# Expert biases of a mixture-of-experts block: copied into the accumulators by ScalarE instead of added by TensorE, GpSimd and VectorE

## The chip, the cores and the metric

One Trainium2 chip, one of its cores in use. The metric is the device time of one launch, in microseconds (us). Engines are named as the profile names them: PE (TensorE), DVE (VectorE), ACT (ScalarE), POOL (GpSimd), SP (SyncE, which here only issues DMAs). PSUM is the memory that PE accumulates into, eight banks of 512 fp32 numbers on each of 128 partitions.

## The reference, cut to what matters

One encoder block on 512 tokens of width 1024: a mixer (recurrent and windowed attention), then a mixture of 32 experts, of which each token takes four. Only the experts matter here. For the rows `x` that an expert `e` receives:

```python
hu = x @ w_up_gate[e] + b_up_gate[e]          # 1024 -> 2048
g, u = hu[:, :1024], hu[:, 1024:]             # gate half, linear half
g = jnp.minimum(g, 7.0)
u = jnp.clip(u, -7.0, 7.0)
act = g * jax.nn.sigmoid(1.702 * g) * (u + 1.0)
y = act @ w_down[e] + b_down[e]
```

All weights are fp32. An expert gets 64 rows on average.

## The kernel before

**Tiles and stages.** The mixer runs until about 540 us of the profiled span, routing and the first expert until about 620 us, and then one expert follows another until about 1706 us. An expert works on 96 row slots (`BLK`). Its weights come as twelve pieces of 128 x 2048 fp32 (1 MB each): eight of `w_up_gate`, four of `w_down`. SP loads each piece into one of six buffers `wraw`; ACT writes its high part, rounded for PE, to `wH` (`high`, L432); DVE writes the rest, raw minus high, to `wL` (`low_piece`, L1756); `wH` and `wL` have four slots each. Each product is then three matmuls, high by high, high by low and low by high (`mm3`, L333 to L335). SP may load the next piece into a buffer when DVE has made the low part of the piece that was there six pieces ago (`load_piece`, semaphore `p_lo`); ACT may overwrite a slot of `wH` when PE has used the piece of four ago (`p_used`).

**PE's order in an expert.** `up_part(i)` accumulates hu in PSUM banks 0 to 3 (96 matmuls of 512 columns), with the eight transposes of the previous expert's activation (`a_part`, L1037) after its second piece; then the transposes of the next expert's rows (`x_part`, L985), and then `down_part(i - 1)`, 48 matmuls into banks 4 and 5. So the up part of an expert is followed by the down part of the expert before it. The order on every engine is the order of the code; a loop covers experts 5 or 6 to 30, the ones ahead and the last one are written out.

**Where the biases are added before.** The gate half's bias lies in `bias` as three bf16 parts of all 32 experts (`bias_high` on ACT and a subtraction on DVE split it once, ahead of the experts). Per expert, DVE writes a matrix `sel` that picks the expert's three rows (`select`, L1852), and `up_part` opens banks 0 and 1 with two bf16 matmuls `sel` by `bias` (L1001, start=True). The linear half's bias comes per expert as two rows of 2 KB (`load_bias_row`, L546), which POOL spreads over 96 partitions of `bias_u` (`spread_bias`, L2203, two PARTITION_BROADCASTs), between its gather of the rows for the expert after next and its scatter of the results of an earlier expert. After the up part, DVE adds the bias and one to the linear half (`clip_up`, L1979, PSUM to `ucl`), and clips `ucl` in place (L1982). ACT takes the gate half through silu (`silu`, L1407) and DVE multiplies the two (`swiglu`, L1989).

**The body on ACT and DVE around the end of an up part.** ACT: the last `high` of expert i, `silu(i)`, `x_high(i + 1)` (L1392), then the `high`s of expert i + 1. DVE: `clip_up(i)`, `select(i + 1)`, one `low_piece`, `swiglu(i)`, `x_low(i + 1)` (L1962), then the `low_piece`s of expert i + 1.

Of the kernel before, what the change touches and what calls it, by code (L numbers as in the profile page):

```python
# [22 lines left out]
BIAS_STEPS = 5  # L47
# [24 lines left out]
K_ID, K_TF, K_TB, K_KF, K_KB, K_REL, K_SL, K_IO, K_LT, K_ON, K_CD, K_P1, K_EPS, K_SE, K_AS, K_TH, K_END = np.cumsum(  # L72
    [0, P, P, P, T, T, 3 * P, QH, NE * NBC, P, P, NE * (NB - 1), 1, 1, NE, NT * TOPK, NB - 1]).tolist()
# [4 lines left out]
def constants():  # L78
# [19 lines left out]
    c[:, K_SE:K_AS] = s % NE == np.arange(NE)[None]  # L98
# [6 lines left out]
def build(nc, x, norm_mix_gain, w_in, hg_lb_fwd, hg_lb_bwd, hg_norm_gain, attn_sink, w_out,  # L105
# [90 lines left out]
    bias = sb("bias", [3 * NE, FF], BF16)  # L196
    brow = sb("brow", [P, FF // 2])
    gd3 = sb("gd3", [P, NT, 3 * NE])
    tab = sb("tab", [P, NE * NBC, 2], I32)
    sel = sb("sel", [3 * NE, P], BF16)  # L200
# [70 lines left out]
    at[0] = small_top + 4 * 2 * FF * 4  # L271
    braw = sb("braw", [3 * NE, FF])
    assert at[0] <= small_top + RAW * 2 * FF * 4

# [56 lines left out]
    def mm3(ps, lh, ll, rh, rl, start, stop):  # L331

        nc.tensor.matmul(ps, lh, rh, start=start, stop=False)  # L333
        nc.tensor.matmul(ps, lh, rl, start=False, stop=False)  # L334
        return nc.tensor.matmul(ps, ll, rh, start=False, stop=stop)  # L335
# [31 lines left out]
    b_in, b_step = sem("b_in"), sem("b_step")  # L367
# [9 lines left out]
    sel_ready = sem("sel_ready")  # L377
# [99 lines left out]
    with nc.Block() as block:  # L477
# [3 lines left out]
        def _(sp):  # L481
# [50 lines left out]
            sp.wait_ge(p_lo, 2)  # L532
            for r in range(3):
                sp.dma_start(braw[r * NE:(r + 1) * NE, :], b_up_gate[0, :, 0:FF]).then_inc(b_in, 16)
# [6 lines left out]
            def load_bias_row(i, e):  # L541
                if not first(i):
                    sp.wait_ge(b_step, BIAS_STEPS + 2 * i)
                for n in range(2):
                    cols = slice(FF + n * FF // 2, FF + (n + 1) * FF // 2)
                    sp.dma_start(brow[32 * n:32 * n + 1, :], b_up_gate[0][bass.ds(e, 1), cols]).then_inc(b_in, 16)  # L546
# [4 lines left out]

            sp.wait_ge(b_step, BIAS_STEPS)
            load_bias_row(0, 0)
            for p in (2, 3):
                load_piece(0, 4 + p, up_src(0, p))
            def load_body(e, begun=0):
                for p in range(begun, 8):
                    load_piece(e, p, up_src(e, p))
                    if p == 1:
                        load_bias_row(e, e)  # L560
                for q in range(4):
                    load_piece(e, 8 + q, down_src(e - 1, q))
# [3 lines left out]
            load_piece(1, 0, up_src(1, 0))  # L566
            load_body(1, 1)
# [9 lines left out]
            with sp.Fori(SETTLED + 1, NE) as e:  # L577
                load_body(e)
            for q in range(4):
                load_piece(NE, q, down_src(NE - 1, q))  # L580
# [16 lines left out]
            def overflow(i, code):  # L597
                e = nc.s_assert_within(code >> NBC_BITS, 0, NE - 1, skip_runtime_bounds_check_because="codes are below NE * NBC")
                sp.wait_ge(x_ready, NT)
                load_bias_row(i, e)  # L600
# [16 lines left out]
        def _(pe):  # L617
# [317 lines left out]

            turn_merged(0)
# [37 lines left out]
            logits(3)  # L974
            first_rows(2)
# [12 lines left out]
            def up_part(i, over=False, turn_last=False):  # L988

                k, b0 = up_at(i, over)  # L990
                if not first(i):
                    pe.wait_ge(ucl_ready, 2 * i - 1)
                    pe.wait_ge(sg_ready, i)
                pe.wait_ge(sel_ready, i + 1)
                if first(i):
                    pe.wait_ge(b_step, BIAS_STEPS)
                    pe.wait_ge(rT_ready, 2 * NT)
                    pe.wait_ge(top_ready, NT)
                    pe.wait_ge(pos_free, 1)
                for n in range(2):  # L1000
                    nc.tensor.matmul(bank[n][0:BLK, :], sel[:, 0:BLK], bias[:, n * 512:(n + 1) * 512], start=True, stop=False)  # L1001
                if not first(i):
                    pe.wait_ge(xTl_ready, 2 * i + KD)
                for p in range(8):
# [4 lines left out]
                    for n in range(4):  # L1009
                        cols = slice(n * 512, (n + 1) * 512)  # L1010
                        last = mm3(bank[n][0:BLK, :], xTH[:, p, :], xTL[:, p, :], wH[:, slot, cols], wL[:, slot, cols], n >= 2 and p == 0, p == 7)
# [1322 lines left out]
```

## Time and profile before

| | us |
|---|---|
| timed runs, median of 3 (lowest to highest) | 1755.31 (1753.12 to 1757.16) |
| profiled execution: span from its first to its last instruction | 1751.3 |
| PE busy in the span | 1724.3 (98%) |
| DVE, ACT, POOL busy | 1441.9, 1140.3, 518.5 |
| one expert in the loop (start of its transposes to the next) | 35.01 |
| DMA in the loop of experts, share of 16 engines | about 0.99 |

The profile gives for its execution only the span; the median of the timed runs is 4.0 us longer, which is what lies around the span (the start, the end, and the spread between runs). In the profile, a matmul's busy time is modelled and overlaps with its neighbours': the distance from one matmul's start to the next is what it costs. An `<-` behind an idle time names what ended it. GB/s are what the 16 DMA engines moved.

### The profile page before, as it was taken

What the parts mean: (1) busy time and instruction counts of PE and PEld (TensorE: products, weight loads), DVE (VectorE), ACT (ScalarE), POOL (GpSimd) and SP (SyncE); (2) the same over time, 40 slices, a digit from 0 to 9 for tenths busy, and PEclk for the clock granted to TensorE, in tenths of its full rate; (3) what the DMA queues carried; (4) which work ended last, traced back from release to release, by engine and by line L of the source; (5) the groups of instructions that cost most, each with busy time, mean ns of one, the idle gap of its engine ahead of it and who ended that gap; (6) DMA issues with size and microseconds to landing.
All of it is one profiled execution on the core that took longest, in us unless ns stands there. A gap on an engine that the chain in (4) does not pass through costs nothing.

```text
span 1751.3 us, 26655 instructions
## 1 busy us (share of the span) xinstructions
PE 1724.3 (98%) x8893; PEld 1275.0 (73%) x8893; DVE 1441.9 (82%) x1489; ACT 1140.3 (65%) x1126; POOL 518.5 (30%) x293
## 2 busy tenths in 40 slices
PE   8999999999999999999999999999999999999997
PEld 7778777777777867677777777777777777777765
DVE  4666676567655889999998999899989998999898
ACT  4544564455454577778777777777777777777783
POOL 1102201210220144223553354334423442344340
PEclk9999999999999999999999999999999999999998
DMA  7431333133125589999999999999999999999985
GB/s 212 145 97 56 88 108 96 48 108 96 48 97 224 189 342 390 352 350 402 382 386 380 370 370 375 382 367 372 377 381 370 368 381 380 368 365 384 381 329 232
DMA packets 159188, 488.19 MB, mean 279 GB/s; under 512 B 13250, under 2 KB 83186, under 8 KB 125744
## 3 DMA queue, kind: packets, MB, share of 16 engines
q1 hardware_dynamic: 151248, 469.03, 72.6%
q0 software_dynamic: 7088, 16.52, 3.0%
q10 hardware_dynamic: 816, 2.19, 0.3%
q8 instruction: 20, 0.33, 0.1%
q14 instruction: 16, 0.13, 0.0%
HBM read 479.17 MB, written 24.39 MB: 288 GB/s over the span
## 4 chain that ended last, share of the span: by engine, by line
PE 92%; DVE 4%; DMA 1%; issue 1%; ACT 1%; DVEq 0%; SPq 0%; ACTq 0%
PE psum L333 27%; PE psum L335 27%; PE psum L334 27%; DVE wL L1756 2%; PE psum L714 1%; PE psum L744 1%; PE psum L1037 1%; PE psum L730 1%; PE psum L985 1%; DMA wraw<-in_w_up_gate 1%; PE psum L680 1%; PE psum L697 1%; PE psum L1001 1%; PE psum L778 0%; ACT wH L432 0%
## 5 line engine op out<-in xcount | busy, mean ns | idle before, releaser
L1756 DVE TENSOR_TENSOR wL<-wraw,wH 128x2048 fp32r<-128x2048 f32 x388 | 880.9, 2293 | 85.1 <-ACT wH L432 84.4
L432 ACT ACTIVATE wH<-wraw 128x2048 fp32r<-128x2048 f32 x388 | 744.5, 1920 | 278.6 <-PE psum L335 264.9
L333 PE MATMUL psum<-wH,xTH 128*96 128x512 f32 x1040 | 416.4, 400 | 2.0 <-DVE wL L1756 1.1
L335 PE MATMUL psum<-wH,xTL 128*96 128x512 f32 x1040 | 408.7, 393 | 0.0
L334 PE MATMUL psum<-wL,xTH 128*96 128x512 f32 x1040 | 408.1, 392 | 0.0
L2203 POOL PARTITION_BROADCAST cst<-brow x64 | 276.3, 4318 | 267.7 <-DMA xg<-x2d,ixg 218.3
L333 PEld LDWEIGHTS psum<-wH,xTH 128*96 128x96 f32 x1040 | 167.9, 161 | 74.7 <-DVE wL L1756 2.6
L335 PEld LDWEIGHTS psum<-wH,xTL 128*96 128x96 f32 x1040 | 167.8, 161 | 72.4
L334 PEld LDWEIGHTS psum<-wL,xTH 128*96 128x96 f32 x1040 | 168.0, 162 | 69.4
L333 PE MATMUL psum<-wH,aTH 128*96 128x512 f32 x496 | 197.0, 397 | 0.0
L335 PE MATMUL psum<-wH,aTL 128*96 128x512 f32 x496 | 195.4, 394 | 0.0
L334 PE MATMUL psum<-wL,aTH 128*96 128x512 f32 x496 | 194.8, 393 | 0.0
L2225 POOL COPY ixg<-tab 128x2 int32 (+1 forms) x31 | 23.2, 750 | 356.6 <-PE psum L985 349.3
L333 PE MATMUL psum<-tsH,xnH 128*128 128x512 f32 (+1 forms) x288 | 112.4, 390 | 0.0
L333 PE MATMUL psum<-xnH,wsH 128*128 128x512 f32 x272 | 109.7, 403 | 1.2 <-DVE xnL L1540 1.2
L335 PE MATMUL psum<-tsH,xnL 128*128 128x512 f32 (+1 forms) x288 | 109.1, 379 | 0.0
L2147 POOL TENSOR_TENSOR qdF<-qp,qdF 128x512 f32<-128x512 f32 x8 | 10.4, 1296 | 333.2 <-DVE dcF L1647 333.2
L334 PE MATMUL psum<-tsL,xnH 128*128 128x512 f32 (+1 forms) x288 | 108.9, 378 | 0.0
L335 PE MATMUL psum<-xnH,wsL 128*128 128x512 f32 x272 | 106.2, 391 | 0.0
L334 PE MATMUL psum<-xnL,wsH 128*128 128x512 f32 x272 | 106.2, 391 | 0.0
L335 PEld LDWEIGHTS psum<-wH,aTL 128*96 128x96 f32 x496 | 80.1, 162 | 34.7
L334 PEld LDWEIGHTS psum<-wL,aTH 128*96 128x96 f32 x496 | 80.4, 162 | 32.8
(273 smaller groups left out, 2264.2 us busy)
## 6 DMA issues: line engine op xcount, KB each, us to landing
wraw<-in_w_up_gate SPq DMA_DIRECT2D x256, 1024.0 KB, 8.2
wraw<-in_w_down SPq DMA_DIRECT2D x128, 1024.0 KB, 7.3
fraw<-in_w_in SPq DMA_DIRECT2D x68, 512.0 KB, 4.1
yd<-in_consts SPq DMA_DIRECT2D x8, 1024.0 KB, 8.0
wraw<-yd SPq DMA_DIRECT2D x3, 2048.0 KB, 9.6
wraw<-in_w_out SPq DMA_DIRECT2D x4, 1024.0 KB
xt<-in_x SPq DMA_DIRECT2D x4, 512.0 KB, 5.5
hres<-in_x SPq DMA_DIRECT2D x4, 512.0 KB, 5.1
```

Source lines behind the costliest of these rows:

```text
L333: nc.tensor.matmul(ps, lh, rh, start=start, stop=False)
L334: nc.tensor.matmul(ps, lh, rl, start=False, stop=False)
L335: return nc.tensor.matmul(ps, ll, rh, start=False, stop=stop)
L432: nc.scalar.activation(wH[:, b % SPLIT, :], raw(b), ACT.Copy).then_inc(p_hi, 1)
L680: last = nc.tensor.matmul(bank[4 + 2 * d + c][:, j * P:(j + 1) * P], kt[rows_of, j, :], vv[rows_of, j, :], start=True, stop=True)
L697: last = nc.tensor.matmul(half, qd[:, tok], S[:, n, :], start=False, stop=True, skip_group_check=True)
L714: nc.tensor.matmul(bank[4 + a][:, 0:len(tiles) * P], aqT[half, n * P:(n + 1) * P], kcur[half, tiles[0] * P:(tiles[-1] + 1) * P], start=Tru ...
L730: last = nc.tensor.transpose(bank[2 + a][:, i * P:(i + 1) * P], sbuf_p[:, a, i * P:(i + 1) * P], ident)
L744: last = nc.tensor.matmul(bank[7][a * DH:(a + 1) * DH, n * P:(n + 1) * P], vcur[:, t, :], pTs[:, a, i, :], start=i == 0, stop=i == len(til ...
L1756: V.tensor_tensor(wL[:, b % SPLIT, :], raw(b), wH[:, b % SPLIT, :].bitcast(F32), ALU.subtract).then_inc(p_lo, 1)
L2203: G.partition_broadcast(bias_u[0:BLK, n * (FF // 2):(n + 1) * (FF // 2)], brow[32 * n:32 * n + 1, :], BLK).then_inc(b_step, 1)
L2225: G.tensor_copy(ixg[:, :], src).then_inc(ix_ready, 1)
```

## The change

- The gate half's three-part bias table, its loads, the ACT copies and DVE subtractions that split it, `sel`, and the two bf16 matmuls of each expert go. So do `brow` and POOL's two PARTITION_BROADCASTs of each expert.
- SP loads each half's bias of an expert by a DMA that writes the same 4 KB row to 96 partitions (384 KB each): `load_gate_bias` to a new tile `bias_g`, `load_up_bias` to `bias_u`. In `load_body(e)` they stand for expert e + 1, ahead of the first and of the second piece of `w_down`.
- ACT copies `bias_g` into banks 0 and 1 (`seed`) and `bias_u` plus one into banks 2 and 3 (`seed_up`), between `x_high(i + 1)` and the next `high`. The up part's matmuls then all accumulate (start=False), and `up_part(i)` waits for the semaphore `seed_ready`.
- DVE's `clip_up` is one instruction that clips from PSUM to `ucl`. Only for expert 0 it still adds bias and one first, since there only the gate half is seeded.
- `mark`, two matmuls of 512 columns on PE, opens banks 0 and 1 once between `logits(3)` and `first_rows(2)`, and `seed(0)` waits for it. `seed_up(1)` takes its bias from `ysb`, loaded on the side.

The diff, cut to its core (what the list says is removed has been left out where its name says enough; in code that runs only when an expert gets over 96 rows the same replacements are made):

```diff
+            def load_gate_bias(i, e):
+
                 if not first(i):
-                    sp.wait_ge(b_step, BIAS_STEPS + 2 * i)
...
+                    sp.wait_ge(seed_ready, 1 if isinstance(i, int) and i == 1 else 2 * (i - 1))
+                sp.dma_start(bias_g[0:BLK, :], b_up_gate[0][bass.ds(e, 1), 0:FF].to_broadcast([BLK, FF])).then_inc(bg_in, 16)
+
+            def load_up_bias(i, e, to=bias_u, free=None, landed=bu_in):
+
+                if free is not None:
+                    sp.wait_ge(*free)
+                sp.dma_start(to[0:BLK, :], b_up_gate[0][bass.ds(e, 1), FF:2 * FF].to_broadcast([BLK, FF])).then_inc(landed, 16)
...
             load_piece(1, 0, up_src(1, 0))
+            load_gate_bias(1, 1)
+            load_up_bias(0, 0, free=(sd1, 2 * NT), landed=bu_first)
+            load_up_bias(1, 1, to=ysb)
             load_body(1, 1)
...
+            def mark():
+
+                for n in range(2):
+                    last = nc.tensor.matmul(bank[n], tri[:, 1, :], tri[:, :, :].rearrange("p a s -> p (a s)").unsqueeze(1).to_broadcast([P, 2, 2 * P]),
+                                            start=True, stop=True)
+                last.then_inc(marked, 1)
...
-                if not first(i):
-                    pe.wait_ge(ucl_ready, 2 * i - 1)
-                    pe.wait_ge(sg_ready, i)
-                pe.wait_ge(sel_ready, i + 1)
...
+                pe.wait_ge(seed_ready, 2 * i + 1)
...
-                for n in range(2):
-                    nc.tensor.matmul(bank[n][0:BLK, :], sel[:, 0:BLK], bias[:, n * 512:(n + 1) * 512], start=True, stop=False)
...
+            def seed(i):
+
+                act.wait_ge(bg_in, 16 * i + 16)
+                if first(i):
+                    act.wait_ge(marked, 1)
+                else:
+                    act.wait_ge(sg_ready, i)
+                A(hu[0:BLK, 0:FF], bias_g[0:BLK, :], ACT.Copy).then_inc(seed_ready, 1)
+
+            def seed_up(i, of=bias_u):
+
+                act.wait_ge(bu_in, 16 * i)
+                act.wait_ge(ucl_ready, 1 if isinstance(i, int) and i == 1 else i + 1)
+                A(hu[0:BLK, FF:2 * FF], of[0:BLK, :], ACT.Identity, bias=cst[0:BLK, K_ON:K_ON + 1]).then_inc(seed_ready, 1)
...
-                dve.wait_ge(b_step, BIAS_STEPS + 2 * i + 2)
-                V.scalar_tensor_tensor(out=ucl[0:BLK, :], in0=hu[0:BLK, FF:2 * FF], scalar=1.0, in1=bias_u[0:BLK, :], op0=ALU.add,
-                                       op1=ALU.add).then_inc(ucl_ready, 1)
-                dve.wait_ge(ucl_ready, 2 * i + 1)
-                V.tensor_scalar(ucl[0:BLK, :], ucl[0:BLK, :], 1.0 + LIMIT, 1.0 - LIMIT, ALU.min, ALU.max).then_inc(ucl_ready, 1)
+                of = hu[0:BLK, FF:2 * FF]
+                if first(i):
+                    dve.wait_ge(bu_first, 16)
+                    V.scalar_tensor_tensor(out=ucl[0:BLK, :], in0=of, scalar=1.0, in1=bias_u[0:BLK, :], op0=ALU.add,
+                                           op1=ALU.add).then_inc(ucl_ready, 1)
+                    dve.wait_ge(ucl_ready, 1)
+                    of = ucl[0:BLK, :]
+                V.tensor_scalar(ucl[0:BLK, :], of, 1.0 + LIMIT, 1.0 - LIMIT, ALU.min, ALU.max).then_inc(ucl_ready, 1)
```

Where instructions stand: line numbers in the rows of the changed kernel are its own (L400 is `high`, L1373 `silu`, L1358 `x_high`, L1379 the evacuation of an expert's result, L1399 `seed`, L1405 `seed_up`, L486 `load_piece`, L510 and L516 the bias loads; `psum` is PSUM, `cst` in L1405 and L516 is the memory of `bias_u`). ACT at the end of an up part, one of the experts written out, before:

```order
L432 ACTIVATE wH<-wraw 128x2048 [waits p_used,wraw_in5]
L1407 ACTIVATE sg<-psum 96x1024 [waits act_ready,p_used]
L1392 ACTIVATE xTH<-psum 128x384 [waits p_used,xT_done]
L1392 ACTIVATE xTH<-psum 128x384 [waits xT_done]
L432 ACTIVATE wH<-wraw 128x2048 [waits p_used,wraw_in0]
L432 ACTIVATE wH<-wraw 128x2048 [waits p_used,wraw_in1]
```

and now:

```order
L400 ACTIVATE wH<-wraw 128x2048 [waits p_used,wraw_in5]
L1373 ACTIVATE sg<-psum 96x1024 [waits act_ready,p_used]
L1358 ACTIVATE xTH<-psum 128x384 [waits p_used,xT_done]
L1358 ACTIVATE xTH<-psum 128x384 [waits xT_done]
L1399 ACTIVATE psum<-bias_g 96x1024 [waits sg_ready,bg_in]
L1405 ACTIVATE psum<-cst 96x1024 [waits ucl_ready,bu_in]
L400 ACTIVATE wH<-wraw 128x2048 [waits p_used,wraw_in0]
L400 ACTIVATE wH<-wraw 128x2048 [waits p_used,wraw_in1]
```

Two instructions stand between the rows of the next expert and its first weight piece. SP's queue around one expert, before:

```order
L518 DMA wraw<-in_w_up_gate 128x2048 [waits p_lo] x2
L546 DMA brow<-in_b_up_gate 1x512 [waits b_step]
L546 DMA brow<-in_b_up_gate 1x512
L518 DMA wraw<-in_w_up_gate 128x2048 [waits p_lo] x6
L518 DMA wraw<-in_w_down 128x2x1024 [waits p_lo] x4
```

and now:

```order
L486 DMA wraw<-in_w_up_gate 128x2048 [waits p_lo] x8
L510 DMA bias_g<-in_b_up_gate 96x1024 [waits seed_ready]
L486 DMA wraw<-in_w_down 128x2x1024 [waits p_lo]
L516 DMA cst<-in_b_up_gate 96x1024 [waits seed_ready]
L486 DMA wraw<-in_w_down 128x2x1024 [waits p_lo] x3
```

The two small loads behind the second up piece are gone, and two loads of 384 KB stand around the first down piece. PE from the last part of routing to expert 0's first product (`hot_150` and `hot_152` are one tile), before:

```order
L884 MATMUL psum<-wr,rT 128x32 x7
L911 MATMUL psum<-hot_152,hres 128x96 [waits h_ready,hot0_ready]
L911 MATMUL psum<-hot_152,hres 128x96 x7
L903 MATMUL psum<-msk,tri 128x32 [waits hot0_ready,mask_ready]
L903 MATMUL psum<-msk,tri 128x32 x3
L896 MATMUL psum<-msk,tri 128x32 [waits hot0_ready,tri_wr_ready,mask_ready]
L896 MATMUL psum<-msk,tri 128x32 x2
L897 MATMUL psum<-msk,tri 128x32
L911 MATMUL psum<-hot_152,hres 128x96 [waits h_ready,hot0_ready]
L911 MATMUL psum<-hot_152,hres 128x96 x7
L1001 MATMUL psum<-bias,sel 96x512 [waits top_ready,rT_ready,pos_free,b_step,sel_ready]
L1001 MATMUL psum<-bias,sel 96x512
```

and now:

```order
L860 MATMUL psum<-wr,rT 128x32 x7
L915 MATMUL psum<-tri 128x512 x2
L887 MATMUL psum<-hot_150,hres 128x96 [waits h_ready,hot0_ready]
L887 MATMUL psum<-hot_150,hres 128x96 x7
L879 MATMUL psum<-msk,tri 128x32 [waits hot0_ready,mask_ready]
L879 MATMUL psum<-msk,tri 128x32 x3
L872 MATMUL psum<-msk,tri 128x32 [waits hot0_ready,tri_wr_ready,mask_ready]
L872 MATMUL psum<-msk,tri 128x32 x2
L873 MATMUL psum<-msk,tri 128x32
L887 MATMUL psum<-hot_150,hres 128x96 [waits h_ready,hot0_ready]
L887 MATMUL psum<-hot_150,hres 128x96 x7
L301 MATMUL psum<-wH,xTH 96x512 [waits xTl_ready,seed_ready,p_lo,pos_free,top_ready]
```

Two matmuls have moved from the start of expert 0 to a place inside routing.

## Rows read from the trace of the kernel before

**Rows 1.** The page: busy time of each engine; the chain that ended last, by engine.

```profile
PE 1724.3 (98%) x8893; PEld 1275.0 (73%) x8893; DVE 1441.9 (82%) x1489; ACT 1140.3 (65%) x1126; POOL 518.5 (30%) x293
...
PE 92%; DVE 4%; DMA 1%; issue 1%; ACT 1%; DVEq 0%; SPq 0%; ACTq 0%
```

**Rows 2.** That chain in order of time, one expert: start, us, what.

```profile
1009.40 0.43 PE psum L1001 x2
...
1015.38 0.66 PE psum L1037 x8
...
1050.39 0.66 PE psum L1037 x8
```

**Rows 3.** Busy us by engine (x instructions) in two stretches, clock, DMA share, GB/s.

```profile
733.80:770.28 36.48, 35.49 (x164) 24.59 (x163) 34.23 (x27) 23.90 (x17) 6.70 (x5) 1.00 0.96 304
...
980.37:1015.38 35.01, 35.01 (x164) 24.76 (x163) 32.01 (x21) 26.25 (x18) 14.38 (x7) 1.00 0.99 379
```

**Rows 4.** Timeline of ACT, end of an up part: start, us, line, operation, [idle before].

```profile
999.52 1.00 ACT L1407 ACTIVATE sg<-psum 96x1024 f32<-96x1024 f32 x1
1000.42 0.86 ACT L1392 ACTIVATE xTH<-psum 128x384 fp32r<-128x384 f32 x2
1001.16 1.92 ACT L432 ACTIVATE wH<-wraw 128x2048 fp32r<-128x2048 f32 x1
1003.90 1.92 ACT L432 ACTIVATE wH<-wraw 128x2048 fp32r<-128x2048 f32 x1 [0.82 <-PE psum L335]
```

**Rows 5.** Timeline of DVE over the same time.

```profile
999.08 1.22 DVE L1979 SCALAR_TENSOR_TENSOR ucl<-psum,cst 96x1024 f32<-96x1024 f32 x1
1000.33 0.69 DVE L1982 TENSOR_SCALAR ucl<-ucl 96x1024 f32<-96x1024 f32 x1
1000.93 0.22 DVE L1852 TENSOR_SCALAR sel<-cst 96x128 bf16 x1
...
1005.34 8.89 DVE L1756 TENSOR_TENSOR wL<-wraw,wH 128x2048 fp32r<-128x2048 f32 x4
```

**Rows 6.** DMA from 757 to 827 us: GB/s in 40 slices, and the sum.

```profile
GB/s 412 410 328 344 417 417 431 421 412 426 398 407 405 426 412 407 421 428 421 417 424 403 323 321 417 412 421 412 393 419 407 410 410 412 421 424 433 421 413 413
DMA packets 5246, 28.47 MB, mean 407 GB/s; under 512 B 613, under 2 KB 613, under 8 KB 2926
```

**Rows 7.** DMA of 21 experts, from 910.34 to 1645.62 us.

```profile
DMA packets 51819, 275.36 MB, mean 374 GB/s; under 512 B 6081, under 2 KB 6081, under 8 KB 30315
```

**Rows 8.** DMA from 632 to 652 us, half a us a slice; an issue, KB, us to landing.

```profile
GB/s 320 164 213 295 336 442 352 410 434 418 451 385 393 410 418 426 418 401 401 442 426 434 434 369 459 393 426 475 344 483 410 377 475 377 459 410 393 459 393 442
...
fgain<-in_final_norm_gain SPq DMA_DIRECT2D x1, 512.0 KB, 10.2
```

**Rows 9.** Timeline of PE at the end of routing and at the start of expert 0.

```profile
590.90 0.18 PE L897 MATMUL psum<-msk,tri 128*128 128x32 bf16 x1
591.69 2.02 PE L911 MATMUL psum<-hot,hres 128*128 128x96 f32 x16 [0.61 <-DVE hot L1840]
593.55 0.60 PE L1001 MATMUL psum<-bias,sel 96*96 96x512 bf16 x2
594.50 0.47 PE L333 MATMUL psum<-wH,xTH 128*96 128x512 f32 x1 [0.35 <-DVE xTL L1846]
```

**Rows 10.** Timelines of PE and of ACT at the start of expert 1.

```profile
622.45 0.47 PE L333 MATMUL psum<-wH,xTH 128*96 128x512 f32 x1 [0.37 <-DVE xTL L1962]
625.70 0.48 PE L333 MATMUL psum<-wH,xTH 128*96 128x512 f32 x1 [0.26 <-DVE wL L1756]
...
620.97 7.33 ACT L432 ACTIVATE wH<-wraw 128x2048 fp32r<-128x2048 f32 x4
```

**Rows 11.** Timelines of DVE and of PE at the end of the last expert.

```profile
1701.96 0.69 DVE L1982 TENSOR_SCALAR ucl<-ucl 96x1024 f32<-96x1024 f32 x1
...
1706.04 1.28 PE L1037 MATMUL psum<-cst,actv 96*128 96x96 f32 x8 [2.19 <-DVE actv L1989]
```

More of the change, by code:

```diff
@@ L46 @@
 BODY = 12
-BIAS_STEPS = 5
 BLK = 96
@@ L195, in build @@
     hres = sb("hres", [P, NT, D])
-    bias = sb("bias", [3 * NE, FF], BF16)
-    brow = sb("brow", [P, FF // 2])
+    bias_g = sb("bias_g", [P, FF])
     gd3 = sb("gd3", [P, NT, 3 * NE])
     tab = sb("tab", [P, NE * NBC, 2], I32)
-    sel = sb("sel", [3 * NE, P], BF16)
     ixg = sb("ixg", [P, 2], I32)
@@ L576, in _ @@
                 sp.dma_start(bdraw[r * NE:(r + 1) * NE, :], b_down[0]).then_inc(bd_in, 16)
-            with sp.Fori(SETTLED + 1, NE) as e:
+            with sp.Fori(SETTLED + 1, NE - 1) as e:
                 load_body(e)
+            load_body(NE - 1, last=True)
             for q in range(4):
@@ L974, in _ @@
             logits(3)
+            mark()
             first_rows(2)
@@ L1010, in up_part @@
                         cols = slice(n * 512, (n + 1) * 512)
-                        last = mm3(bank[n][0:BLK, :], xTH[:, p, :], xTL[:, p, :], wH[:, slot, cols], wL[:, slot, cols], n >= 2 and p == 0, p == 7)
+                        last = mm3(bank[n][0:BLK, :], xTH[:, p, :], xTL[:, p, :], wH[:, slot, cols], wL[:, slot, cols], first(i) and n >= 2 and p == 0, p == 7, seeded=n < 2 or not first(i))
                     last.then_inc(p_used, 1)
@@ L1323, in _ @@
             merged_high(7)
-            def bias_high(n):
-                left = (3 - n) * NE
-                if n == 0:
-                    act.wait_ge(b_in, 16 * 3)
-                else:
-                    act.wait_ge(b_step, 2 * n)
-                A(bias[0:left, :], braw[0:left, :], ACT.Copy).then_inc(b_step, 1)
-            for n in range(3):
-                bias_high(n)
             def rows_out(j):
@@ L1437, in _ @@
             x_high(1, used(up_at(0), 8))
+            seed(1)
+            seed_up(1, ysb)
             high(act, 1, 1)
@@ L1467, in body @@
                     x_high(i + 1, used((i, 0), 8))
+                    seed(i + 1)
+                    seed_up(i + 1)
                 high(act, i + 1, 0)
@@ L1491, in overflow @@
                 x_high(i, used((i, 0), 0))
+                seed(i)
+                seed_up(i)
                 for p in range(8):
@@ L1781, in _ @@
             merged_low(7)
-            for n in range(2):
-                left = (2 - n) * NE
-                dve.wait_ge(b_step, 2 * n + 1)
-                V.tensor_tensor(braw[0:left, :], braw[0:left, :], bias[0:left, :], ALU.subtract).then_inc(b_step, 1)
             step = [0]
@@ L1860, in _ @@
             scaled_rows(1)
-            select(0)
             add_rows(2)
@@ L2008, in _ @@
             clip_up(0)
-            select(1)
             x_low(1)
@@ L2030, in body @@
                 clip_up(i)
-                if prefetch:
-                    select(i + 1)
                 low_piece(i, 11)
@@ L2088, in overflow @@
             def overflow(i, code):
-                e = nc.s_assert_within(code >> NBC_BITS, 0, NE - 1, skip_runtime_bounds_check_because="codes are below NE * NBC")
-                select(e)
                 x_low(i)
```

90 lines of the change are left out of this document (19 added, 71 removed).

## The prediction, made before the run

> **What bounds the kernel now.** I read the page's busy times first, then the chain, and then one expert on each engine. PE is busy in 98% of the span and carries 92% of the chain that ended last [rows 1]. Followed in order of time, the chain in the loop of experts is PE and nothing else: from one expert's transposes (1015.38) to the next one's (1050.39) are 35.01 us without a gap, and in them stands one piece of 0.43 us, the two bias matmuls of L1001 [rows 2]. The stretch of the same length before it shows PE busy for 35.01 of 35.01 us at full clock (1.00, the level of 2.4 GHz), DVE 32.01, ACT 26.25 [rows 3]. So in this stage only what PE executes counts, as long as no other engine comes to the bound. The one that is nearest is not DVE but the DMA: its share is 0.99 there, although the rate, 379 GB/s, is below the 407 that it reached from 757 to 827 us [rows 3, 6]. The reader should keep these two facts apart: PE is the bound, and the change hands work from PE to the resource behind it.
>
> **The change, part by part.** (1) *The two bias matmuls.* They leave 29 experts (2 to 30) in the PE-bound stage: 29 x 0.43 = 12.5 us less [rows 2]. Expert 0's two stand in front of a wait of 0.35 us for x that stays, and are worth next to nothing [rows 9]; experts 1 and 31 are taken below.
>
> (2) *The two copies on ACT.* No row shows ACT writing PSUM. The nearest is silu, which reads PSUM for the same 96 x 1024 in 1.00 us [rows 4]; I take 1.0 each, with 0.9 and 1.2 as likely ends and 2 as a far one. They stand between x_high and the next high, which so moves from 1001.16 to about 1003.2 and ends at 1005.1. DVE gets to that piece's low part at 1005.34 [rows 5], so this `low_piece` isn't later, ends at about 1007.6 as before, and PE wants it at 1009.4, where its up part begins [rows 2]. The next high starts at 1003.90 after an idle of 0.82 us and is pushed to 1005.1, the one after it by less, and by the fourth ACT is back in step with PE: this cover is about 1.8 us, and the copies cost nothing until both together take over 3.8 us. `seed_up` makes ACT wait for the clip, with all further highs queued behind: the clip begins at 999.08 and needs at most 1.22 [rows 5], so it is done at 1000.3, and ACT gets there at 1002.2. PE's own new wait, for the copies, ends six us before it matters.
>
> (3) *VectorE.* The add (1.22) and the clip (0.69) become one clip that reads PSUM, and select (0.22) goes [rows 5]. Between a PSUM read at 1.22 and an SBUF read at 0.69 I take 1.22, the row that reads PSUM over the same shape: 0.9 us less an expert, all beside PE. It tells on the path only at the end, where PE waits 2.19 us for the last expert's product behind that clip [rows 11]: 0.7 less there (0 to 1.2). The Trainium skill ("VectorE: DVE Perf Modes", section "Why PSUM operands drop a tier") says that a PSUM operand keeps fp32 at the plain rate: by it, too, the clip loses the pace of its 0.69, and by the other reading, 0.69, the end would give 1.2.
>
> (4) *GpSimd.* Its spreading stands off PE's path; the scatter behind it comes earlier, and nothing waits for that before the end of the experts. Costed at nothing. The same for the one-time split of the bias table, which lies beside PE's output projection; at most it would give back ACT's three copies, some 3 us, an estimate from the 1.00 of rows 4.
>
> (5) *The loads.* 2 x 96 x 4 KB = 0.79 MB more per expert. Now an expert moves 275.36 / 21 = 13.11 MB [rows 7]; at 407 GB/s, the rate of a stretch with work always queued [rows 6], that is 32.2 us. With 0.79 MB, 13.90 MB take 34.15 us, against a PE period of 35.01 - 0.43 = 34.58. So they fit, with 0.4 us to spare in each expert. A load that writes one row to all partitions isn't dear by itself: `fgain`, 512 KB from one row, was issued at 635 us and landed after 10.2, and in the slices up to 645 the rate stays near 400 or above [rows 8]. The dear kind is the gather: in rows 6 it shows as two dips (328 344 and 323 321, beside about 414; slices of 1.75 us), each some 0.3 MB lost on top of the 0.26 MB that it moves, 2.1 times its bytes. If the bias loads behaved so, they would take 4.1 us instead of 1.9. These two are the ends; I take the first, since `fgain` is the same kind of load. SP's waits in front of them are for copies of an expert whose pieces it has already issued, so no weight load queues behind an open wait.
>
> The Trainium skill speaks against adding loads at all ("DMA: Bandwidth & Descriptors", section "Where 436 GB/s comes from"): for transfers from HBM it puts a core's limit at about 358 GB/s. By it the loop could not run as it does, and 13.90 MB would take 38.8 us, an estimate from that page. The 374 GB/s of rows 7 and the 407 of rows 6 disagree with it, so the measurement decides; only a trace of chance is left to that rule.
>
> (6) *The front.* `mark` puts two matmuls, 0.43 by L1001, ahead of `first_rows(2)`, the `totals` and the positions at 590.90; DVE's 0.61 us behind them is on the path [rows 9], so all of it is: +0.4 (0 to 0.6). Expert 1 has no down part in front of it, so nothing covers its copies: ACT's four highs that began at 620.97 back to back begin 2 us later, the second piece's high ends at 624.9, its low part at 627.2, and PE, which got that piece at 625.70 [rows 10], gets it then: +1.6 (1.0 to 2.0).
>
> (7) *The stretch from 733.80.* One expert took 36.48 there, 1.5 over the others [rows 3], when small transfers stand in SP's queue and pieces arrive late. With less room on the DMA the lag is caught up later, and the first dips after it can stop PE: +1.5 (-1 to +4; a gain if DVE's 0.9 shortens the stretch).
>
> Sum: -12.5 - 0.7 + 0.4 + 1.6 + 1.5 = -9.7, so a span of 1741.6 for this profiled execution. The median of the timed runs is 4.0 above its span of 1751.3; I keep that distance: **1745.6 us**.
>
> **The rivals.** *A: the DMA sets the pace, just under PE's old one.* It needs a load pair that costs between 2.4 and 2.8 us, or a rate under 402. For it: one expert of the loop has a rate of 379 and yet a share of 0.99 [rows 3], and dips are not filled when buffers are short. Against it: 407 held over two experts. Taken at 34.85 us an expert, it gives back 0.27 x 29 = 7.8 of the 12.5: about 1753.4; between 34.65 and 35.0 us an expert it is 1748 to 1758.
>
> *B, slower: the DMA sets the pace above the old one.* The place is the same queue: twelve pieces, one gather, one scatter and now two loads for an expert. It decides from a pair over 35.01 - 32.2 = 2.8 us, 1.5 times its bytes at 407. At the gather's 2.1 times (4.1 us) an expert takes 36.3: 1.3 x 29 = +38, and with the front's and the stretch's +3.5 and the end's -0.7 it is 1796; at the deciding point it is 1758. ACT would then wait for `wraw` in every expert. For it speaks that the loads reach 96 partitions as the gather does; against it, `fgain`. By the page's 358 in place of 407 the slowdown would be larger, 3.8 us an expert; the same rival by another cause.
>
> *C: the copies are slow.* If each takes over 1.9 us, PE waits for the first piece at each up part. At 2.2 each, 4.4 together, 0.6 us an expert come back, more than the 0.43 saved: 0.17 x 29 = +5, with the +2.8 of the rest 1763. Nothing in the trace has ACT so slow on 96 x 1024.
>
> **How the numbers follow.** The forecast 0.55, A 0.24, B 0.14 (0.02 of it the page's rule), C 0.07. The range should leave out B past its start and the worst of C: from 1740 (mark hidden, the end at -1.2, the stretch at -1, runs 2 us below their median) to 1759 (A at its upper end, the stretch at +4). A measurement of this kernel can tell some 0.2%, 3.5 us, from no change: faster is below 1751.8, slower above 1758.8. The forecast is faster but for its edge (0.53 and 0.02 same); of A 0.11 is faster and 0.13 the same; of B 0.13 slower and 0.01 the same; of C 0.02 faster, 0.02 the same, 0.03 slower. So faster 0.66, same 0.18, slower 0.16.
>
> **What would show it.** Right: PE without a gap at 34.6 us an expert, no L1001 in the chain; the two copies at about 1.0 us each between x_high and the next high, with the first low part still at its old place; a DMA rate near 402 GB/s in the loop and ACT waiting for `wraw` hardly at all after about 900 us; the first matmul of expert 1 later by a us or two. Wrong: ACT's waits for `wraw` in every expert and PE waiting for `wL` (A or B, told apart by the period against 35.01); copies over 1.9 us (C); a period under 34.5 would mean that matmuls which accumulate from the start are cheaper, which nothing here shows.

## The result, and the profile after

The changed kernel takes 1853.2 us (median; 1850.6 to 1868.5), the kernel before 1754.8 beside it: a ratio of 1.058, 95% interval 1.056 to 1.060. It is 98 us slower; the forecast was 1745.6. The profiled execution has a span of 1851.3, so 100.0 more than the 1751.3 of before.

The page of the changed kernel, answering [rows 1]: busy time by engine, the chain that ended last by engine and by line, and the two groups of instructions that handle the raw weights (busy us and mean ns of one, then idle time before them and what ended it).

```profile
PE 1738.9 (94%) x8831; PEld 1264.5 (68%) x8831; DVE 1412.9 (76%) x1424; ACT 1191.3 (64%) x1186; POOL 256.1 (14%) x229
...
DMA 38%; PE 37%; DVE 11%; ACT 7%; issue 6%; SPq 1%; ACTq 0%; DVEq 0%
...
L1744 DVE TENSOR_TENSOR wL<-wraw,wH 128x2048 fp32r<-128x2048 f32 x388 | 879.2, 2289 | 209.8 <-ACT wH L400 209.1
L400 ACT ACTIVATE wH<-wraw 128x2048 fp32r<-128x2048 f32 x388 | 739.1, 1915 | 324.3 <-DMA wraw<-in_w_down 175.4
```

No engine has become busier in a way that matters: DVE and POOL lost work, ACT gained 51 us over 32 experts, and PE shows 15 us more with 62 matmuls fewer, in a busy time that is modelled. But the chain, 92% PE before, is now 38% DMA. The waits say the same piece by piece (us in total, times, longest us):

```profile
DVE wL L1744 <- ACT wH L400: 209.1, 211, 3.5
ACT wH L400 <- DMA wraw<-in_w_down: 175.4, 113, 4.5
PEld psum L301 <- DVE wL L1744: 126.8, 103, 3.9
ACT wH L400 <- DMA wraw<-in_w_up_gate: 109.1, 132, 3.0
PE psum L301 <- DVE wL L1744: 82.8, 71, 3.4
```

ACT waits for raw weights 245 times, some eight to an expert, 284.5 us in all; in the whole run before it was 12 times and 12.5 us:

```profile
ACT wH L432 <- DMA wraw<-in_w_up_gate: 9.1, 8, 2.9
ACT wH L432 <- DMA wraw<-in_w_down: 3.4, 4, 1.7
```

DVE waits for ACT, PE for DVE. A piece of the chain in order of time shows the same links (start, us, what):

```profile
1092.11 2.30 DVE wL L1744
1094.43 0.04 SPq L486
...
1094.56 16.11 DMA wraw<-in_w_down
...
1110.77 1.92 ACT wH L400
...
1112.72 2.33 DVE wL L1744
...
1115.20 12.40 DMA wraw<-in_w_up_gate
```

DVE frees a buffer, SP issues the next piece at once, and that piece takes 16.11 us to land; then ACT and DVE handle it and the next issue follows. The page's list of DMA issues (KB each, median us to landing) has this for all of them, before (the first two lines) and after:

```profile
wraw<-in_w_up_gate SPq DMA_DIRECT2D x256, 1024.0 KB, 8.2
wraw<-in_w_down SPq DMA_DIRECT2D x128, 1024.0 KB, 7.3
...
wraw<-in_w_up_gate SPq DMA_DIRECT2D x256, 1024.0 KB, 12.5
wraw<-in_w_down SPq DMA_DIRECT2D x128, 1024.0 KB, 16.4
...
bias_g<-in_b_up_gate SPq DMA_DIRECT2D x32, 384.0 KB, 13.3
cst<-in_b_up_gate SPq DMA_DIRECT2D x31, 384.0 KB, 15.8
```

Stretches, answering [rows 3] (columns as there; the last two are DMA share and GB/s): 400 us before, the same 400 us after, and one expert after.

```profile
1000.00:1400.00 400.00, 400.00 (x1848) 282.76 (x1847) 366.57 (x232) 300.46 (x207) 158.48 (x68) 1.00 0.99 373
...
1000.00:1400.00 400.00, 370.68 (x1674) 254.25 (x1674) 330.66 (x192) 296.92 (x214) 57.79 (x41) 1.00 1.00 365
1081.56:1119.34 37.78, 35.25 (x162) 24.27 (x161) 31.26 (x19) 27.98 (x22) 5.06 (x4) 1.00 1.00 366
```

After, PE is busy for 93% of the stretch, at full clock. The DMA engines are never free (share 1.00), and yet they move 365 GB/s, less than the 373 of before, where PE had no gap, and far less than 407 [rows 6]. From 1005.33 to 1386.32 ten gate copies of ACT lie 38.10 us apart on average, where an expert took 35.01: 3.1 us for each of some thirty experts makes 93 of the 100 us. (Below, "an expert" is always this distance between gate copies, over 8 to 11 experts past 1000 us.)

ACT and DVE at the end of an up part, answering [rows 4, 5]:

```profile
1079.92 1.00 ACT L1373 ACTIVATE sg<-psum 96x1024 f32<-96x1024 f32 x1
1080.82 0.85 ACT L1358 ACTIVATE xTH<-psum 128x384 fp32r<-128x384 f32 x2
1081.56 1.03 ACT L1399 ACTIVATE psum<-bias_g 96x1024 f32<-96x1024 f32 x1
1082.51 1.12 ACT L1405 ACTIVATE psum<-cst 96x1024 f32<-96x1024 f32 x1
```

```profile
1079.72 1.22 DVE L1962 TENSOR_SCALAR ucl<-psum 96x1024 f32<-96x1024 f32 x1
```

The copies (1.03 and 1.12) and the clip (1.22) are what the prediction took them for. So the suspicion falls on the two bias loads. The experiments ask first whether they are the whole of it, then what makes them dear.

### The profile page after: what moved, and what is told of

Same layout as the page of the kernel before. It is cut to its first block, busy times and chain, and to the rows that moved or that the text cites. A ratio compares the mean times of both kernels' runs of the same rounds, so it can differ in the third digit from the quotient of the medians.

```text
span 1851.3 us, 26206 instructions
## 1 busy us (share of the span) xinstructions
PE 1738.9 (94%) x8831; PEld 1264.5 (68%) x8831; DVE 1412.9 (76%) x1424; ACT 1191.3 (64%) x1186; POOL 256.1 (14%) x229
## 3 DMA queue, kind: packets, MB, share of 16 engines
q10 hardware_dynamic: 816, 2.19, 0.3%
## 4 chain that ended last, share of the span: by engine, by line
DMA 38%; PE 37%; DVE 11%; ACT 7%; issue 6%; SPq 1%; ACTq 0%; DVEq 0%
DMA wraw<-in_w_down 25%; DMA wraw<-in_w_up_gate 12%; PE psum L301 10%; PE psum L303 9%; PE psum L302 9%; DVE wL L1744 9%; ACT wH L400 5%; PE psum L690 1%; PE psum L720 1%; PE psum L706 1%; PE psum L656 1%; PE psum L673 1%; ACT sg L1373 1%; ACT psum L1399 1%; PE psum L754 0%
## 5 line engine op out<-in xcount | busy, mean ns | idle before, releaser
L400 ACT ACTIVATE wH<-wraw 128x2048 fp32r<-128x2048 f32 x388 | 739.1, 1915 | 324.3 <-DMA wraw<-in_w_down 175.4
L301 PE MATMUL psum<-wH,aTH 128*96 128x512 f32 x496 | 202.3, 408 | 36.5 <-DVE wL L1744 33.7
L301 PEld LDWEIGHTS psum<-wH,aTH 128*96 128x96 f32 x496 | 80.2, 162 | 94.1 <-DVE wL L1744 65.5
L2192 POOL COPY ixs<-tab 128x2 int32 (+1 forms) x30 | 37.7, 1258 | 523.9 <-issue 482.9
L1523 DVE TENSOR_TENSOR wsL<-fraw,wsH 128x1024 fp32r<-128x1024 f32 x34 | 49.2, 1448 | 43.8 <-ACT wsH L1135 43.2
## 6 DMA issues: line engine op xcount, KB each, us to landing
wraw<-in_w_up_gate SPq DMA_DIRECT2D x256, 1024.0 KB, 12.5
wraw<-in_w_down SPq DMA_DIRECT2D x128, 1024.0 KB, 16.4
```

Source lines behind the costliest of these rows:

```text
L301: nc.tensor.matmul(ps, lh, rh, start=start, stop=False, skip_group_check=seeded)
L400: nc.scalar.activation(wH[:, b % SPLIT, :], raw(b), ACT.Copy).then_inc(p_hi, 1)
L1523: V.tensor_tensor(out_, raw, high.bitcast(F32), ALU.subtract).then_inc(w_lo, 1)
L2192: G.tensor_copy(ixs[:, :], src).then_inc(ixs_ready, 1)
```

## The experiments

The theories. L: the loads' transfers are all of the loss. Of what makes them dear, P: they write 96 partitions, where the weight pieces write 128; R: each reads one row of memory 96 times. As rivals, O: not the transfers but the new order (waits in SP's queue, ACT's copies); F: any further load at this place costs that. (The later expectations name theories of their own by letters; theory F of the fourth experiment group is another than the F here.) Unless a section says otherwise, the edit is to these two lines of the changed kernel (`load_gate_bias`, `load_up_bias`):

```diff
 sp.dma_start(bias_g[0:BLK, :], b_up_gate[0][bass.ds(e, 1), 0:FF].to_broadcast([BLK, FF])).then_inc(bg_in, 16)
...
 sp.dma_start(to[0:BLK, :], b_up_gate[0][bass.ds(e, 1), FF:2 * FF].to_broadcast([BLK, FF])).then_inc(landed, 16)
```

### Loads of one row

```diff
-sp.dma_start(bias_g[0:BLK, :], ....to_broadcast([BLK, FF]))
+rows = BLK if isinstance(i, int) and i == 0 else 1
+sp.dma_start(bias_g[0:rows, :], ....to_broadcast([rows, FF]))
```

> The changed kernel with its loads cut: from expert 1 on (for the up half from expert 2) a bias load fills one partition of 96 (4 KB), so 95 rows keep expert 0's (or 1's) bias; all instructions, copies, clips, waits and queues stay. This leaves out the spreading of the bias. If the loads' transfers alone are the cause of 1853 us (theory L), every other step of the prediction stands and the time is 1743 to 1747 us, with an expert every 34.6 us and ScalarE's waits for raw weights back at before's level. If the cause lies in the order (SP's new waits, ScalarE's copies, VectorE's clip; theory O), it stays within 10 us of 1853 us and an expert takes 37.5 us or more.

Measured: 1743.7 us (1741.7 to 1746.6), ratio to before 0.994 (0.992 to 0.995). The page's chain and the ten-expert stretch of this kernel:

```profile
PE 94%; DVE 3%; ACT 1%; issue 1%; DMA 1%; SPq 0%; DVEq 0%; ACTq 0%
```

```profile
1000.00:1400.00 400.00, 400.00 (x1857) 284.40 (x1856) 362.75 (x209) 324.56 (x233) 95.67 (x48) 1.00 0.98 378
```

PE is busy for 400.00 of 400.00 us, and an expert takes 34.57. O falls; the loads are the whole of the loss, and all the rest of the change is worth 11 us.

### 128 partitions, 96 other rows, 128 other rows

Three kernels fill the square of theories P and R: the same row to 128 partitions, 96 different rows to 96 partitions, 128 different rows to 128.

```diff
-bias_g[0:BLK, :], b_up_gate[0][bass.ds(e, 1), 0:FF].to_broadcast([BLK, FF])
+bias_g[0:P, :], b_up_gate[0][bass.ds(e, 1), 0:FF].to_broadcast([P, FF])
...
+bias_g[0:BLK, :], w_down[0][bass.ds(e, 1), 0:BLK, 0:FF].rearrange("o p n -> (o p) n")
...
+bias_g[0:P, :], w_down[0][bass.ds(e, 1), 0:P, 0:FF].rearrange("o p n -> (o p) n")
```

> The changed kernel with both bias loads written to 128 partitions instead of 96, each still 128 copies of one 4 KB row; the pair is 1.05 MB instead of 0.79. Theory P (a destination of 96 partitions, 6 rows for each of 16 DMA engines, lies badly against the 128-row weight pieces): now 13.11 + 1.05 = 14.16 MB at the 407 GB/s of [rows 6] is 34.8 us for an expert, 1745 to 1760 us in all. Theory R (reading one row of memory over and over is what is dear, about 5.6 us for 96 copies): 128 copies cost 7.5 us, an expert 39.7 us, 1905 us in all.

> The changed kernel with both bias loads taken from 96 different rows of the expert's down weights (4 KB each, same bytes, same 96 partitions, same queue and place) instead of 96 times the bias row; so the bias added is a wrong one, nothing else changes. Theory P (96 partitions): as the change, 1853 us, an expert every 37.8 us. Theory R (one row read again and again): 13.90 MB at 407 GB/s, 34.2 us, so an expert every 34.6 us and 1743 to 1750 us.

> The changed kernel with both bias loads taken from 128 different rows of the down weights and written to 128 partitions (wrong biases, otherwise the same work): two loads of the kind of the weight pieces, half as long a row. By theory P and by theory R alike 14.16 MB at 407 GB/s, 34.8 us for an expert, 1745 to 1760 us. If any further load at this place costs over 5 us, whatever its rows (theory F: rows of 4 KB, or two more loads in the queue), it is 1853 us or more.

Measured: 1780.0, 1861.4 and 1774.1 us; an expert 35.81, 39.00 and 35.61. R falls: with rows of their own 96 partitions cost as much as with one row (1861 against 1853), and 128 as much as 128 (1774 against 1780). F falls, since two full loads are far cheaper. What is left is P: **a third more bytes to 128 partitions is 73 us cheaper than 96.** The ten-expert stretch of the kernel with the same row to 128:

```profile
1000.00:1400.00 400.00, 388.71 (x1786) 272.92 (x1785) 345.29 (x200) 308.10 (x222) 86.35 (x44) 1.00 1.01 396
```

The DMA engines are as full as after the change, but move 396 GB/s (398 with rows of their own). In the kernel with 96 other rows they move 358:

```profile
1000.00:1400.00 400.00, 364.58 (x1637) 249.17 (x1638) 320.64 (x186) 288.57 (x208) 56.84 (x42) 1.00 1.01 358
```

Still the two kernels with 128 rows miss what was expected of them at 407 GB/s (1745 to 1760): 396 to 398 is what this mix of loads gets.

### 64 and 112 partitions, and the gate half alone

> The changed kernel with both bias loads cut to the first 64 partitions from expert 1 on (for the up half from expert 2); the other 32 rows keep expert 0's or 1's bias, so their spreading is left out. Without the loads an expert's 13.11 MB take 32.8 us at the 397 to 400 GB/s that the 128-row runs showed; 96 rows twice cost 5.0 us on top (37.8 measured), 128 rows twice 2.9 us (35.6 to 35.8). Theory A, every load to fewer than 128 partitions is slow by its bytes (5.0 us for 0.79 MB): 0.52 MB is 3.3 us, an expert 36.1 us, 1790 us in all. Theory C, it is slow by how unevenly it falls on partitions 0 to 63 and 64 to 127 (96 rows: 64 against 32, 3.0 us over its bytes): 64 against 0 is 6.0 + 1.3 us, an expert 40 us, 1905 us. Bytes alone: 34.1 us, PE's own 34.57 us decides, 1744 us. The Trainium skill (SBUF — State Buffer, section on the DMA port swizzle) has 64 partitions reach half of the ports, so that 64 rows would take as long as 128: 2.9 us, 35.7 us an expert, 1778 us.

> The changed kernel with both bias loads written to 112 partitions (from expert 1 on, the up half from expert 2), the values the reference's. Theory A (anything under 128 partitions is slow by its bytes): 0.92 MB at 5.0 us for 0.79 is 5.8 us, an expert 38.6 us, 1864 us. Theory C (unevenness between the halves of the partitions, here 64 against 48): 1.5 + 2.3 us, an expert 36.6 us, 1803 us. Bytes alone: 2.3 us, 35.1 us, 1760 us.

> The changed kernel with the gate half's load as it is (96 partitions) and the up half's cut to one partition of 4 KB from expert 2 on (95 rows keep expert 1's bias; their spreading is left out). If each load has its own price (theories A and C), one is half of 5.0 us: 32.8 + 2.5 = 35.3 us for an expert, 1765 us in all. If one such load puts the queues out of step for all that follows (theory D), one is nearly as bad as two: 37 us or more for an expert, 1820 to 1850 us.

The edits put 64 or 112 for the row count above, or leave the gate load at 96 and cut the up load to 1. Measured: 64 rows 1855.9 us (an expert 38.47), 112 rows 1872.1 (39.25), one load of 96 1787.1 (1779 to 1795; 35.53). No theory had the 64 rows right: they cost as much as 96, with two thirds of the bytes. A's 1864 for 112 came nearest. One load costs about half of two (35.53 less 33.1 us for the rest is 2.4, of the pair's 5.0; the table below has the working), so D falls. The stretch with 64 rows shows the DMA full at its lowest rate:

```profile
1000.00:1400.00 400.00, 369.03 (x1652) 251.24 (x1653) 326.23 (x190) 293.45 (x211) 55.51 (x42) 1.00 1.01 357
```

### 64 rows on every second partition, and 32 rows

```diff
-bias_g[0:BLK, :], ....to_broadcast([BLK, FF])
+bias_g[0:P:2, :], ....to_broadcast([P // 2, FF])
```

> The changed kernel with both bias loads written to 64 partitions, every second one of 128 (0, 2, 4, ...), from expert 1 on (the up half from expert 2); the odd rows keep an older bias, so half of the spreading is left out. The 64 rows 0 to 63 cost as much as 96 (1856 us). Theory E, any load that isn't of 128 rows costs that, wherever it lands: 1845 to 1870 us. Theory F, what costs is that the rows crowd on a part of the partitions: 64 rows spread evenly over all of them cost their bytes (0.52 MB at 397 GB/s, 1.3 us, an expert 34.57 us by PE) up to what 128 rows cost (2.9 us, 35.7 us): 1744 to 1780 us.

> The changed kernel with both bias loads cut to the first 32 partitions from expert 1 on (the up half from expert 2); the other rows keep an older bias, so their spreading is left out. If each load that isn't of 128 rows has a fixed price (64 and 96 rows: some 5 us the pair): an expert 37.5 to 38 us, 1845 to 1860 us. If the price goes by the rows that crowd on the first partitions (64 rows 5.4 us, so 32 rows 2.7 us): 32.8 + 2.7 = 35.5 us, 1772 us. Bytes alone: 0.7 us, 1744 us.

Measured: 64 rows on every second partition 1746.1 us (1743.3 to 1749.9), an expert 34.57; 32 rows in one block 1773.2, an expert 35.29. A fixed price for every load that isn't of 128 rows (1845 to 1860) falls with both.

```profile
1000.00:1400.00 400.00, 400.00 (x1855) 283.71 (x1854) 362.73 (x210) 324.46 (x234) 94.13 (x48) 1.00 1.00 395
```

Beside the row of the block of 64 above: the same count of loads, rows and bytes, in the same place of the queue, and 395 GB/s in place of 357, PE without a gap in place of 369 of 400 us. Only where the rows land differs, and it is worth 110 us. So E falls, and theory P becomes more exact: **where the rows land makes them dear, not how many they are.** That the crowding on a part of the partitions is the reason (this expectation's F) fits the 64 rows; the 112 rows, which lie on nearly all partitions and cost the most, speak against it as the whole reason. The Trainium skill ("SBUF — State Buffer", section "Door 1: The DMA port swizzle") has partitions 0 to 63 reach half of the ports through which DMAs write SBUF. The direction agrees with these runs. Its size doesn't: by its 218 GB/s for 64 partitions the pair of 64 rows would take 2.4 us (an estimate from that page), and the runs give some 5.4, the 38.47 less 33.1 for the rest (13.11 MB at 396 GB/s).

### The same bytes, spread evenly

```diff
-sp.dma_start(bias_g[0:BLK, :], ....to_broadcast([BLK, FF])).then_inc(bg_in, 16)
+for r in range(3):
+    sp.dma_start(bias_g[r:P:4, :], ....to_broadcast([P // 4, FF])).then_inc(bg_in, 16)
```

> The changed kernel with each of its two bias loads split into three of 32 rows, written to every fourth of the 128 partitions (0, 4, ...; 1, 5, ...; 2, 6, ...): the same 0.79 MB for an expert as the change, in the same queue and place, but spread evenly over all partitions; partitions 3, 7, ... keep an older bias, so a quarter of the rows isn't the reference's. By crowding (64 rows in one block 1856 us, every second partition 1746): the loads cost their bytes, 13.90 MB at the 397 GB/s of the 128-row runs is 35.0 us for an expert, 1757 us (1750 to 1765). If rows that are fewer than 128 cost for themselves, or six loads cost more than two, it is 1775 us or more.

Measured: 1764.8 us (1763.7 to 1765.8), ratio 1.0055 (1.0037 to 1.0074); an expert 35.24.

```profile
1000.00:1400.00 400.00, 395.21 (x1819) 277.58 (x1818) 350.27 (x203) 312.79 (x224) 82.15 (x46) 1.00 1.01 395
```

It lies at the upper edge of what was expected by crowding alone, and it divides the loss. From 1743.7 to 1764.8 are **21 us for the bytes** (an expert from 34.57 to 35.24: 13.90 MB at 395 GB/s), from there to 1853.2 are **88 us for where they land** (from 35.24 to 38.10). The kernel has six loads where the change has two; if the splitting itself costs something, the first part is smaller and the second larger.

### ScalarE's queue, and one load of 128

> The changed kernel with both bias loads as they are (96 partitions), but issued by ScalarE into its own queue, from expert 2 on, right after the seeds that read the tiles, instead of by SP among the weight pieces. If the loads are dear because their rows compete with the weights' rows at the destination, the queue changes nothing: 1840 to 1865 us. If they are dear because the weights stand behind them in one queue (SP's), what is left is their bytes: 13.90 MB at 397 GB/s, 35.0 us, 1757 us, and up to 1 us an expert more for the issuing on ScalarE (1757 to 1787 us).

> The changed kernel with the gate half's load written to 128 partitions and the up half's cut to one partition of 4 KB from expert 2 on (95 rows keep expert 1's bias, their spreading is left out). One load to 96 partitions instead gave 1787 us. If a load to 128 partitions costs its bytes, 13.11 + 0.52 = 13.63 MB at 397 GB/s are 34.3 us, under PE's 34.57: 1743 to 1749 us. If it costs half of what the pair showed over PE's period (35.7 against 34.57), 35.1 us and 1760 us.

For the first, SP's two calls in `load_body` go, and ACT issues the loads for expert i + 2 after the first `high` of expert i + 1:

```diff
+act.wait_ge(seed_ready, 2 * k - 1)
+act.dma_start(bias_g[0:BLK, :], ....to_broadcast([BLK, FF])).then_inc(bg_in, 16)
+act.dma_start(bias_u[0:BLK, :], ....to_broadcast([BLK, FF])).then_inc(bu_in, 16)
```

Measured: 1818.5 us (1814 to 1823), an expert 37.07: between the two expectations. Most of the price stays with the rows wherever they are issued, but 35 us go. The Trainium skill ("DMA: Bandwidth & Descriptors", section "Issuing engines are not separate DMA queues") says that another issuing engine saves only the time of issuing; here it saved 1 us an expert. Whether that is the queue or the moment (the pair issued right behind the copies that read the tiles, not among the pieces), this run doesn't tell.

One load of 128 rows: 1749.6 us (1746.5 to 1752.7), ratio 0.997 (0.995 to 0.9995), an expert 34.87. The DMA moves 391 GB/s there, and PE is busy for 398.95 of 400 us. At 396 GB/s the 13.63 MB would take 34.4 us, just under PE's 34.57; it lies a little over the first expectation, and a load of 128 rows costs little but not nothing.

### A version with both gains: rows of 2 KB, spread by GpSimd

```diff
+for n in range(4):
+    sp.dma_start(brow[32 * n:32 * n + 1, :], b_up_gate[0][bass.ds(e, 1), n * FF // 2:(n + 1) * FF // 2]).then_inc(b_in, 16)
...
+for n in range(4):
+    to = (bias_g, bias_u)[n // 2][0:BLK, (n % 2) * (FF // 2):(n % 2 + 1) * (FF // 2)]
+    G.partition_broadcast(to, brow[32 * n:32 * n + 1, :], BLK).then_inc(sp_step, 1)
```

> A version with the same seeding by ScalarE and the same single clip, but from expert 2 on the two halves' bias comes as four loads of 2 KB to one partition each and is spread to 96 partitions by GpSimd (four spreads for an expert where the kernel before had two), after the gather and ahead of the scatter. If the shape and size of the two big loads is the whole loss, an expert takes PE's own 34.57 us and the time is 1743 to 1750 us, 0.3 to 0.7% under the kernel before. If GpSimd's spreads come too late for the seeds (each of 2.5 to 7.5 us before, so up to 30 us for four, against some 35 us from seed to seed), or hold up VectorE, an expert takes over 35 us and the time is 1757 us or more.

Measured: 1747.4 us (1743.9 to 1750.3), ratio to before **0.995 (0.993 to 0.997)**; an expert 34.57. GpSimd in one expert:

```profile
1053.93 2.87 POOL L2226 PARTITION_BROADCAST bias_g<-brow  x1 [8.42 <-DMA xg<-x2d,ixg]
1056.96 2.50 POOL L2226 PARTITION_BROADCAST bias_g<-brow  x1 [0.16 <-POOL bias_g L2226]
1059.63 2.50 POOL L2226 PARTITION_BROADCAST cst<-brow  x1 [0.16 <-POOL bias_g L2226]
1062.30 0.80 POOL L2226 PARTITION_BROADCAST cst<-brow  x1 [0.16 <-POOL cst L2226]
```

Four spreads end at 1063.1, well ahead of the next gate copy at 1077.88, on an engine that is busy for less than half of the time (195.26 of the 400 us). This version keeps the change's seeds and its single clip and is 8 to 9 us faster than the kernel before.

The runs whose two loads copy the bias row, side by side; "cost of the pair" is an estimate, an expert less 33.1 us (13.11 MB at 396 GB/s), worked out where the DMA set the pace:

| bias loads, per half | MB an expert | median us | us an expert | cost of the pair, us |
|---|---|---|---|---|
| 1 row | 0.01 | 1743.7 | 34.57 | (PE sets the pace) |
| 64 rows, every second partition | 0.52 | 1746.1 | 34.57 | 1.5 or less |
| 32 rows in a block | 0.26 | 1773.2 | 35.29 | 2.2 |
| 96 rows, three of four partitions | 0.79 | 1764.8 | 35.24 | 2.1 |
| 128 rows | 1.05 | 1780.0 | 35.81 | 2.7 |
| 64 rows in a block | 0.52 | 1855.9 | 38.47 | 5.4 |
| 96 rows in a block (the change) | 0.79 | 1853.2 | 38.10 | 5.0 |
| 112 rows in a block | 0.92 | 1872.1 | 39.25 | 6.1 |

## Why the prediction was wrong, by its own steps

**(1) The bias matmuls: right.** With the loads gone an expert takes 34.57, as 35.01 - 0.43 has it.

**(2) The copies and (3) the clip: right** in size (1.03, 1.12, 1.22), and covered: in the one-row kernel PE is busy in all of the stretch. At the end of the last expert PE's wait went from 2.19 [rows 11] to 1.39 in the one-row kernel, 0.8 where 0.7 was taken.

**(4) GpSimd at nothing: right.** Putting its spreads back, and two more, leaves an expert at 34.57.

**(5) The loads: the step that failed.** It is the term of 1.9 us for the pair, by which the loads fit with 0.4 us to spare and cost nothing, and it failed twice. First the rate. 407 GB/s was read from one stretch of 70 us [rows 6]; over 400 us, with the DMA never free, the runs without narrow blocks get 391 to 398. At 395, 13.90 MB are 35.2 us, over PE's 34.57, and even well spread loads cost 21 us. Rival A asked the right question (a rate under 402), but the answer already lies past its upper end of 35.0 us, on B's side. Second, and larger, the analogy. `fgain` [rows 8] was taken as the same kind of load because it too copies one row to many partitions. But it writes 128 partitions, and what the runs show to count is where the rows land, not where they come from. In place of 1.9 us the pair cost 5.0 by the table, beyond the 4.1 (2.1 times its bytes, as the gather) that the step had named as the far end. The row for that end was there: the gather writes 96 partitions and cost twice its bytes (that its price has the same cause is not shown). The prediction named it under rival B and let `fgain` speak against it; taking the row whose destination is the same would have given 36.3 us an expert and 1796, slower. B, with a chance of 0.14, named the mechanism's place and its sign; its price was 57 us short of the 1853.2.

The rule of the Trainium skill that the step weighed ("DMA: Bandwidth & Descriptors", section "Where 436 GB/s comes from": about 358 GB/s from HBM for a core) was not the cause. The changed kernel's 365 lies near it, but the same bytes spread evenly moved at 395.

**(6) The front: mark right, expert 1 short where the clock fell.** In the changed kernel the first product of expert 0 comes 1.9 us later than before (594.50 in [rows 9]):

```profile
596.37 0.45 PE L301 MATMUL psum<-wH,xTH 128*96 128x512 f32 x1 [0.99 <-DVE xTL L1829]
```

Of this, 1.5 lies ahead of the mark, which starts at 590.19 where before `first_rows(2)` started at 588.73; no term of the prediction had it, and it differs between runs (with 128 other rows the positions come at 590.60, before at 590.90). The mark and the longer wait for x are the rest, 0.4 together. Expert 1's price shows without the loads' disturbance in the one-row kernel. On PE in order of time (L1407 is `seed_up` in this kernel), and then the 5 us behind the wait, in this kernel and in the kernel before (columns as in [rows 3]):

```profile
623.02 0.88 PE L971 MATMUL psum<-cst,xg 96*128 96x96 f32 x8 [0.17 <-DMA xg<-x2d,ixg]
...
626.84 0.73 PE L301 MATMUL psum<-wH,xTH 128*96 128x512 f32 x1 [2.94 <-ACT psum L1407]
...
627.00:632.00 5.00, 5.00 (x12) 3.27 (x13) 3.53 (x2) 5.00 (x3) 0.00 (x0) 0.50 0.17 52
...
627.00:632.00 5.00, 5.00 (x29) 3.66 (x28) 5.00 (x3) 3.97 (x4) 5.00 (x1) 1.00 0.94 362
```

From silu of expert 0 to that of expert 1 it takes 31.54 us where before took 28.62: 2.9 in place of 1.6. The prediction had followed the delayed `high`s there, and not PE's own new wait for the copies, which is covered in every expert but this one. The wait of 2.94 us is not itself the 2.9: before, PE waited 2.1 in the same place, in three pieces (1.51, 0.37, 0.26). Behind the longer wait the granted clock is 0.50, the level of 1.2 GHz, and PE does 12 matmuls in the 5 us where before it did 29. With one load of 128 rows the same wait is 3.33 us, the clock stays at 1.00 and silu to silu is 30.17, 1.6 more than before. So the forecast had the size that shows without the fall of the clock; the fall is the rest.

**(7) The stretch from 733.80: near.** In the one-row kernel the experts there take 2.3 us over three periods (38.63, 33.86, 33.56 against 34.57), before took 1.4 over (36.12, 36.76, 33.60 against 35.01): 0.9 more where 1.5 was forecast.

Without the loads the time is 1743.7 where the prediction said 1745.6, but so near partly by luck. In the profiled execution of the one-row kernel the front and expert 1 cost 6.5 us (silu of expert 1 at 654.43, before at 647.93) where 2.0 was forecast, and its span, 1743.6, is 7.7 below the 1751.3 of before where 9.7 was forecast. And its time, 1745.5, lies 1.9 above its span: half of the 4.0 that the prediction kept was the spread between runs. All of the miss of 108 us is still one term that had been set to zero because it fitted by 0.4 us.

## What to carry to other kernels

When an edit hands work to a resource that is already at 0.99 of its time, price it by the row whose destination and shape are the same, and let the far bound decide the sign when the slack is 1%. A DMA to 64, 96 or 112 partitions in a block isn't cheaper than one to 128: beside full-width loads, writing all 128, or the same rows spread over them, or single rows that another engine spreads, took less time here. Before adding bytes, test the idea with the load cut to one row: it parts the engines' share of an edit from the DMA's in one run.

## What the runs showed of the hardware that was not expected

- 64 rows of 4 KB to partitions 0 to 63, twice an expert, cost 5.4 us; the same 64 to every second partition at most 1.5. 112 in a block cost 6.1, more than 128 (2.7), though the fullest half holds 64 rows in both. So more than the fuller half's share is at work; which part of the chip makes it, and why the full 128 in a block is cheap for its bytes, these runs don't settle.
- A busy share of 1.00 of the DMA engines can mean 357 GB/s or 396. The time of a weight piece to landing doesn't tell the two apart so well: it rises from 8.2 us (up) and 7.3 (down) to 12.5 and 16.4 after the change, but to 12.3 and 14.1 with 128 rows too, at 396 GB/s.
- A `PARTITION_BROADCAST` of 2 KB to 96 partitions took 2.1 us on average (four an expert), where before the same took 4.3 (two an expert; from 1000 to 1400 us the first of them 5.1 to 7.5 us, the second 2.5). The place among the other engines' work had changed; the reason was not tested.
